# A two-layer decoder trunk: gating-unit projections moved ahead of the queries, four statistics moved in TensorE's queue, layer norm of the convolution one attention step earlier

## The chip, the cores and the metric

The kernel runs on one core of one Trainium2 chip. The metric is device time in microseconds of one execution. Before the change it is 2908.12 us, the median of three runs that lie between 2907.37 and 2908.25 us.

## What is computed

Two layers, each on 512 positions of width 1024, in fp32. Cut to what matters here:

```python
h = h + 0.5 * swiglu(rms(h), ffn1)
z = rms(h) @ w_in                      # one projection: columns for all mixers and gates
A = silu(layer_norm(causal_conv31(a * sigmoid(g)))) @ conv_out        # 512 channels
B = (u * (tril(ws) @ rms(v) + b)) @ sgu_out,   u, v = split(gelu(z_sgu))   # "gating unit"
C = nsa(z_q, z_kv, z_ngate) @ nsa_out  # 8 heads of 64, queries and keys RMS-normed,
                                       # three branches weighted by sigmoid(z_ngate)
h = h + (sig(g_A)*A + sig(g_B)*B + sig(g_C)*C) @ w_out
h = h + cross_attention(rms(h), rms(mem))
h = h + 0.5 * swiglu(rms(h), ffn2)
```

Everything lies transposed on the chip (channels on partitions, the 512 positions along the free side), so a statistic over channels is a matmul with a matrix of ones (`ones`, or `bdon` for heads of 64).

## The kernel before

**Units.** Every projection is cut into "units", one per 128 output columns: SP loads 1024 x 128 weights into `raw` (2 buffers), ScalarE copies their high part (`wH`, line 1083), GpSimd subtracts to get the low part (`wL`, line 563), TensorE does 24 matmuls of 512 columns (high x high, high x low, low x high for 8 slices, lines 616, 619 and 622; 12 for units with 4 slices), and VectorE takes the result out of one of 4 PSUM banks (`scaled`, line 1422, times the inverse RMS). ScalarE's `ahead(l, u)` prepares unit u + 3 as soon as unit u - 1 is done. The order of units within a layer is a table of offsets: `U_KV` (6 units), `U_CONV` (6), `U_QP` (4, the queries in pairs of heads), `U_NG` (2 half units, the gates of the attention branches), `U_SGU` (8: v then u of the gating unit), `U_CONV2` (2), and then `U_G`: 24 branch units (12 matmuls each) alternating with 24 gate units (24 matmuls each).

**Queues.** Each engine has a program in order, written out by hand in one block per engine (TensorE line 603, ScalarE line 1079, VectorE line 1412, GpSimd line 519, SP line 355). They are tied by counting semaphores: `stat_in` says that the squares for a statistic lie in `sacc`, `stat_mm` that TensorE has summed them, `stat_rt` that ScalarE has taken the root, `st_mm`/`st_out` count transposes on TensorE and their copies on ScalarE, `s_mm`/`s_out` scores and their readers on VectorE, `q_ok` normed queries, `vn` the normed v.

**Chain of a norm.** VectorE squares a tile into `sacc` (`squares`, line 1555), TensorE sums it (`stat`, line 628), ScalarE takes the root (`root`, line 1122), VectorE takes the reciprocal (`root_of`, line 1428) and multiplies (`normed`, line 1560). `sacc` and `rv` exist once, so these chains go one behind another. For v of the gating unit ScalarE makes the squares, TensorE sums the four of them (`v_squares`, line 759), and VectorE norms four tiles of 128 x 512 (line 1680).

**Pieces between matmuls.** From `U_CONV2` on, TensorE puts small work between the matmuls of the units. In the first four of these units `opening(p)` (line 890) is called after every 4 matmuls: transposes of v (`v_turned`), the mixing matmuls of the gating unit (`mixed`), the first scores. After that `attention(i, p)` (line 902) is called after every 2 matmuls, p = 0 to 17 within step i (branch unit i - 1 and gate unit i + 1): scores of step i, and transposes (`turned`) and value products (`values`) of step i - 1. There are 16 steps. Step i - 1 has 5, 2, 4 or 3 groups of transposes in turn.

**The order around the change.** ScalarE in step i: prepare a unit, copy out transposes 0 of step i - 1, the exponentials of half 0 of step i, copy out transposes 1, prepare a unit, and so on. VectorE in step i: row maxima of half 0 (`maxes`), the gate unit, convolution taps, maxima of half 1, the branch unit, weights (`weigh`), more taps. The convolution has 4 tiles of 31 taps: one is done by GpSimd (lines 577 to 594), the other three by VectorE (`conv(count)`, line 1593), where two of them accumulate in PSUM until their last taps. In steps 6 to 8 VectorE and ScalarE do the layer norm of the convolution: sum at step 6, mean taken off, squares and sum at step 7, root, reciprocal and product at step 8, then Silu and the high copies on ScalarE at the end of step 8, and `low("A", 4)` on VectorE; branch unit 8, which opens step 9, needs them.

Of the kernel before, what the change touches and what calls it, by code (L numbers as in the profile page):

```python
# [12 lines left out]
P = 128  # L13
# [4 lines left out]
def trunk(nc, x, mem, norm_ffn1, ffn1_wi, ffn1_wo, norm_mix, w_in, conv_w, conv_b, conv_ln_g,  # L18
# [38 lines left out]
    U_QP = U_CONV + 6  # L57
    U_NG = U_QP + 4
    U_SGU = U_NG + 2
    U_CONV2 = U_SGU + 8  # L60
# [10 lines left out]
    with ctx:  # L71
# [160 lines left out]
        def rows_of(u):  # L232
            if U_NG <= u < U_SGU or U_XO <= u < U_F2:
# [100 lines left out]
        q_ok = sig("q_ok", 1)  # L334
# [20 lines left out]
        def _(sp):  # L355
# [80 lines left out]
            with sp.Fori(0, L) as l:  # L436
# [13 lines left out]

                def pair_cols(j):
# [21 lines left out]
                for j in range(4):  # L473
                    unit(l, U_SGU + j, 0, cols_of(win, C_SGU + DS + j * P))
                for j in range(4):
                    unit(l, U_SGU + 4 + j, 0, cols_of(win, C_SGU + j * P))
# [42 lines left out]
        def _(pool):  # L519
# [52 lines left out]
            with pool.Fori(0, L) as l:  # L572
                lows(l, 0, U_QP)
# [3 lines left out]
                for u in range(U_QP, U_WO):  # L577
# [25 lines left out]
        def _(pe):  # L603
# [24 lines left out]
            def stat(l, s, weights, n=T):  # L628

                pe.wait_ge(stat_in, risen(stat_in, l, s + 1 if s < 9 else s))  # L630
# [56 lines left out]
            with pe.Fori(0, L) as l:  # L687
# [55 lines left out]
                unit(l, U_QP, 0, KD, gH, gL)  # L743
                for j in range(1, PAIRS):
                    unit(l, U_QP + j, 0, KD, gH, gL)
                    if j >= 2:
                        stat(l, 3 + j, bdon)
                for i in range(2):
                    unit(l, U_NG + i, 0, 4, lambda k: gxH[:, 4 * i + k, :],
                         lambda k: gxL[:, 4 * i + k, :])  # L750
                stat(l, 7, bdon)
                unit(l, U_SGU, 0, KD, gH, gL)

                pe.wait_ge(t_free, risen(t_free, l, 3))
                pe.wait_ge(ng_sig, risen(ng_sig, l, 1))
                for a in range(TT):
                    last = turn(pT[:, a * P:(a + 1) * P], hb[:, a * P:(a + 1) * P])
                last.then_inc(ng_tr, 1)
                def v_squares(k):
                    if k == 0:  # L760
                        pe.wait_ge(stat_rt, risen(stat_rt, l, 9))
# [4 lines left out]
                for j in range(1, 8):  # L766
                    unit(l, U_SGU + j, 0, KD, gH, gL)
                    if j == 1:
                        stat(l, 8, bdon)
                    if 2 <= j < 6:  # L770
                        v_squares(j - 2)


                def v_turned(c):
                    if c == 0:
                        pe.wait_ge(vn, risen(vn, l, 1))
                        pe.wait_ge(t_free, risen(t_free, l, 4))
# [6 lines left out]
                def mixed(c):  # L784

                    pe.wait_ge(sg_cp, risen(sg_cp, l, c + 1))
                    if c:
                        pe.wait_ge(sg_out, risen(sg_out, l, c))
# [6 lines left out]
                def scores(key):  # L795
# [3 lines left out]
                    else:  # L799
                        pe.wait_ge(q_ok, risen(q_ok, l, 1))  # L800
                    if isinstance(key, str):
                        j = int(key[1:])
                        for c in range(TT):
# [98 lines left out]
                def attention(i, p):  # L902
                    a, n = p // 3, len(groups(i - 1))
                    if p % 3 == 0:
                        if a < n:
                            turned(i - 1, a)
                        elif a == 5 and i == 6:
                            middle("mean", 10)
                        elif a == 5 and i == 7:
                            middle("var", 11)  # L910
# [5 lines left out]
                    elif 1 <= a <= n:  # L916
                        values(i - 1, a - 1)
# [161 lines left out]
        def _(act):  # L1079
# [72 lines left out]
            with act.Fori(0, L) as l:  # L1152
# [38 lines left out]
                ahead(l, U_QP)  # L1191
                for j in range(1, PAIRS):
                    ahead(l, U_QP + j)
                    if j >= 2:
                        root(l, 3 + j, rv, 1.0 / DH)
                ahead(l, U_NG)
                ahead(l, U_NG + 1)
                act.wait_ge(ng_in, risen(ng_in, l, 1))
                act.activation(hb, sr, ACT.Sigmoid).then_inc(ng_sig, 1)
                root(l, 7, rv, 1.0 / DH)  # L1200
                for j in range(8):
# [4 lines left out]
                    if j == 1:  # L1206
                        root(l, 8, rv, 1.0 / DH)
# [6 lines left out]
                    if j == 5:  # L1214
                        root(l, 9, rv, 1.0 / DS)
# [61 lines left out]
                exps_c(0)  # L1277
                v_out(3)
                exps(0, 0)
                ahead(l, gate_unit(0))  # L1280
# [9 lines left out]
                for i in range(1, NS + 1):  # L1290
# [13 lines left out]
                    ahead(l, branch_unit_of(i - 1))  # L1304
                    turned_out(i - 1, 0)
# [4 lines left out]
                    turned_out(i - 1, 1)  # L1310
                    ahead(l, gate_unit(i + 1))
# [9 lines left out]
                    if i == 6:  # L1321
                        act.wait_ge(st_mm, risen(st_mm, l, STEP["mean"] + 1))
                        copy(sil, pT, scale=-1.0 / DC).then_inc(st_out, 1)
                    if i == 7:
                        act.wait_ge(st_mm, risen(st_mm, l, STEP["var"] + 1))
                        act.activation(rv[:, :], pT, ACT.Sqrt, bias=eps[:, 0:1],
                                       scale=1.0 / DC).then_inc(st_out, 1)
                    if i == 8:
# [83 lines left out]
        def _(dve):  # L1412
# [116 lines left out]
            with dve.Fori(0, L) as l:  # L1529
# [109 lines left out]

                scaled(qT[:, 0, :], l, U_QP)  # L1640
                squares(qT[:, 0, :])
                conv(4)
                for j in range(1, PAIRS):
                    scaled(qT[:, j, :], l, U_QP + j)
                    if j >= 2:
                        normed(l, 3 + j, qT[:, j - 2, :], g8[:, j - 2:j - 1])
                        squares(qT[:, j - 1, :])
                    conv(3 if j == 1 else 1)
# [5 lines left out]
                normed(l, 7, qT[:, 2, :], g8[:, 2:3])  # L1654
                squares(qT[:, 3, :])
                conv(3)


                for j in range(8):
                    if j >= 2:  # L1660
                        dve.wait_ge(gelu, risen(gelu, l, j - 1))
                    scaled(tb[:, j % 2, :], l, U_SGU + j)
                    if j == 0:
                        dve.wait_ge(ng_tr, risen(ng_tr, l, 1))
                        dve.tensor_copy(gates[:, :, :], pT[:, :].rearrange("p (a c) -> p a c", a=4)
# [331 lines left out]
```

## Time and profile before

| what | value |
|---|---|
| median of the runs | 2908.12 us |
| the profiled execution | 2897.9 us, its span 2896.2 us |
| TensorE matmul busy | 2737.8 us (95%) |
| VectorE busy | 1213.8 us (42%) |
| ScalarE busy | 1159.7 us (40%) |
| GpSimd busy | 1223.7 us (42%) |

The profiled execution is 10.2 us below the median of the others. Times in rows are microseconds from the start of its span; in lines of the timeline the first number is the start, the second the duration, then engine, line, operation, the tiles written and read, and the count; in brackets how long the engine sat idle before it and what released it. PE is TensorE, DVE VectorE, ACT ScalarE, POOL GpSimd. The stretch in question lies at 476 to 800 us in the first layer and, 1430 us later, again in the second.

### The profile page before, as it was taken

The page shows a single profiled execution, that of the slowest core. Times are in us where ns is not written, and L with a number is a line of the kernel's source. Part 1 is how long each engine was busy: PE and PEld are TensorE (multiplying, and loading weights), DVE is VectorE, ACT ScalarE, POOL GpSimd, SP SyncE. Part 2 cuts the span into 40 slices and gives each one's busy share as a digit, 9 for nine tenths or more (in the row PEclk, how much of TensorE's full clock was granted, in tenths as well). Part 3 has the DMA queues.
Part 4 walks back from the last instruction along what each step waited for, and adds up shares of the span by engine and source line. Part 5 has one row for each costly group of instructions (what it writes and reads, how often), then busy time and mean ns, then how long its engine had stood idle before and what let it go on. Part 6 is the DMA issues. An engine that isn't in the chain of part 4 may idle for free.

```text
span 2896.2 us, 39971 instructions
## 1 busy us (share of the span) xinstructions
PE 2737.8 (95%) x13192; PEld 2153.7 (74%) x13192; DVE 1213.8 (42%) x1781; ACT 1159.7 (40%) x1682; POOL 1223.7 (42%) x624
## 2 busy tenths in 40 slices
PE   6999999899899989999999999998998999899999
PEld 5888877665567777888878888776555677688887
DVE  5222265776334554121242212667863346531212
ACT  4322332366764334222352223324667543342221
POOL 3443445752224424444444444467422344244443
PEclk8999999999999999999999999999999999999999
DMA  3335333221124313333333353332111332133332
GB/s 105 102 95 127 98 88 80 70 56 44 44 56 113 95 37 103 101 94 95 95 88 102 94 131 88 88 80 59 55 45 44 80 99 84 55 102 95 95 101 80
DMA packets 493189, 243.69 MB, mean 84 GB/s; under 512 B 49528, under 2 KB 491234, under 8 KB 493026
## 3 DMA queue, kind: packets, MB, share of 16 engines
q1 hardware_dynamic: 493026, 241.62, 30.0%
q8 instruction: 89, 1.46, 0.2%
q14 instruction: 74, 0.61, 0.1%
HBM read 239.46 MB, written 2.10 MB: 83 GB/s over the span
## 4 chain that ended last, share of the span: by engine, by line
issue 56%; POOL 25%; PE 12%; POOLq 7%; DVE 0%; DVEq 0%
POOL wL L563 24%; PE pg L616 4%; PE pg L619 4%; PE pg L622 4%; POOLq L589 3%; POOLq L591 3%; POOL wsn L587 1%; POOLq L562 1%; POOLq L568 0%; DVE big L1968 0%; POOL convb L584 0%; DVE xT L1475 0%; PE pg L667 0%; DVEq L71 0%; POOL tab L547 0%
## 5 line engine op out<-in xcount | busy, mean ns | idle before, releaser
L563 POOL TENSOR_TENSOR wL<-raw,wH 128x1024 fp32r<-128x1024 f32 (+1 forms) x480 | 1085.1, 2262 | 1637.2 <-ACT wH L1083 1634.2
L616 PE MATMUL pg<-gxH,wH 128*128 128x512 f32 x2320 | 938.0, 404 | 29.5 <-DVE gxL L1438 25.3
L622 PE MATMUL pg<-gxH,wL 128*128 128x512 f32 x2320 | 917.9, 396 | 0.0
L619 PE MATMUL pg<-gxL,wH 128*128 128x512 f32 x2320 | 916.1, 395 | 0.0
L1083 ACT ACTIVATE wH<-raw 128x1024 fp32r<-128x1024 f32 (+1 forms) x480 | 475.7, 991 | 487.7 <-PE pg L622 352.5
L616 PEld LDWEIGHTS pg<-gxH,wH 128*128 128x128 f32 x2320 | 440.0, 190 | 146.3 <-DVE gxL L1438 28.7
L619 PEld LDWEIGHTS pg<-gxL,wH 128*128 128x128 f32 x2320 | 440.5, 190 | 104.8 <-issue 18.8
L622 PEld LDWEIGHTS pg<-gxH,wL 128*128 128x128 f32 x2320 | 439.8, 190 | 94.6 <-issue 4.5
L616 PE MATMUL pg<-hH,wH 128*128 128x512 f32 (+1 forms) x1184 | 456.7, 386 | 20.7 <-DVE hL L1778 20.7
L622 PE MATMUL pg<-hH,wL 128*128 128x512 f32 (+1 forms) x1184 | 455.9, 385 | 0.0
L619 PE MATMUL pg<-hL,wH 128*128 128x512 f32 (+1 forms) x1184 | 454.0, 383 | 0.0
L616 PEld LDWEIGHTS pg<-hH,wH 128*128 128x128 f32 x1184 | 225.9, 191 | 64.9 <-DVE hL L1778 22.4
L1475 DVE SCALAR_TENSOR_TENSOR xT<-pg,xT 128x512 f32<-128x512 f32 x128 | 88.4, 691 | 432.3 <-PE pg L622 432.3
L619 PEld LDWEIGHTS pg<-hL,wH 128*128 128x128 f32 x1184 | 225.4, 190 | 55.2 <-issue 14.4
L622 PEld LDWEIGHTS pg<-hH,wL 128*128 128x128 f32 x1184 | 225.7, 191 | 37.8
L1083 ACT ACTIVATE hH<-tmp 128x512 f32 x88 | 55.6, 632 | 305.1 <-DVE tmp L1490 305.1
L1490 DVE TENSOR_TENSOR tmp<-pg,tmp 128x512 f32<-128x512 f32 x88 | 60.9, 692 | 255.1 <-PE pg L622 252.7
L1485 DVE TENSOR_TENSOR tb<-pg,rstd 128x512 f32<-128x512 f32 x88 | 60.8, 690 | 247.3 <-PE pg L622 245.9
L1136 ACT ACTIVATE tmp<-tb 128x512 f32<-128x512 f32 x88 | 55.5, 631 | 259.9 <-DVE tb L1485 259.9
L1241 ACT ACTIVATE prob<-prob,nb 128x512 f32<-128x512 f32 (+3 forms) x128 | 70.9, 555 | 91.6 <-DVE nb L1740 91.4
L1494 DVE TENSOR_TENSOR hL<-tmp,hH 128x512 f32 x88 | 70.0, 796 | 82.5 <-ACT hH L1083 82.5
L1487 DVE TENSOR_TENSOR tmp<-tmp,rstd 128x512 f32<-128x512 f32 x88 | 72.0, 818 | 74.1 <-ACT tmp L1136 74.1
(214 smaller groups left out, 2180.0 us busy)
## 6 DMA issues: line engine op xcount, KB each, us to landing
raw<-in_ffn_wi SPq DMA_DIRECT2D x352, 256.0 KB, 3.1
raw<-in_w_in SPq DMA_DIRECT2D x200, 256.0 KB, 3.2
raw<-in_ffn_wo SPq DMA_DIRECT2D x128, 256.0 KB, 3.0
raw<-in_ffn_wo SPq DMA_DIRECT2D x64, 192.0 KB, 2.6
raw<-in_w_out SPq DMA_DIRECT2D x32, 256.0 KB, 3.1
raw<-in_xkv SPq DMA_DIRECT2D x32, 256.0 KB, 3.1
raw<-in_sgu_out SPq DMA_DIRECT2D x32, 128.0 KB, 2.2
raw<-in_conv_out SPq DMA_DIRECT2D x32, 128.0 KB, 2.2
```

What stands on the lines that cost most here:

```text
L563: pool.tensor_tensor(wL[:, s % 4, 0:n, :], raw[:, s % 2, 0:n, :], wH[:, s % 4, 0:n, :].bitcast(F32), ALU.subtract)\
L589: pool.drain()
L591: pool.drain()
L616: mm(o, wH[:, s, k, :], rh(k), start=(k == 0), stop=False)
L619: mm(o, wH[:, s, k, :], rl(k), start=False, stop=False)
L622: last = mm(o, wL[:, s, k, :], rh(k), start=False, stop=(k == kt - 1))
L1083: return act.activation(o, i, ACT.Copy, **kw)
L1241: act.activation(t, t, ACT.Exp, bias=nb[:, s % 2, b, e:e + 1], scale=-1.0, accum_out=dn[:, s % 2, b, e:e + 1])
L1475: STT(xT[:, k, :], bank, by, xT[:, k, :], ALU.mult, ALU.add).then_inc(evac, 1)
L1487: TTt(sr, sil, rstd[:, :], ALU.mult)
L1490: TTt(hb, bank, sr, ALU.mult).then_inc(evac, 1)
L1494: TTt(hL[:, slot, :].rearrange(flat), hb, hH[:, slot, :].rearrange(flat).bitcast(F32), ALU.subtract).then_inc(hid_l, 1)
```

## The change

Nothing is computed differently. The eight units of the gating unit now stand ahead of the four query units. The v statistic becomes the first of this stretch; the statistics of the query pairs follow their projections one pair later, the last one as a piece of `opening`. The transposed branch gates also become a piece of `opening`. VectorE's queue follows: the norm of v comes right behind query unit 0, the norm of query pair 2 opens the stretch behind the gates, and that of pair 3 stands behind `weigh_c(0)`, with four taps, ahead of step 1. The taps are 5 instead of 4 at a time in steps 1 to 4. In the layer norm the sum moves to the end of step 5, the mean and squares to the end of step 6, reciprocal and product to step 7, Silu and the high copies to the end of ScalarE's step 7, `low("A", 4)` to the middle of VectorE's step 8. On TensorE the matmul of the mean stands at p = 6 of step 6, that of the variance at p = 0 of step 7, ahead of that step's transposes, which all move up by three pieces.

```diff
-    U_QP = U_CONV + 6
+    U_SGU = U_CONV + 6
+    U_QP = U_SGU + 8
     U_NG = U_QP + 4
-    U_SGU = U_NG + 2
-    U_CONV2 = U_SGU + 8
+    U_CONV2 = U_NG + 2
...
         for i in range(1, NS + 1):
+            if i == 7:
+                order.append("var")
             for g in range(len(groups(i - 1))):
...
-            if i == 7:
-                order.append("var")
...
-        q_ok = sig("q_ok", 1)
+        q_ok = sig("q_ok", PAIRS)
...
# TensorE
+                unit(l, U_SGU, 0, KD, gH, gL)
...
+                for j in range(1, 8):
+                    unit(l, U_SGU + j, 0, KD, gH, gL)
+                    if 3 <= j < 7:
+                        v_squares(j - 3)
                 unit(l, U_QP, 0, KD, gH, gL)
                 for j in range(1, PAIRS):
                     unit(l, U_QP + j, 0, KD, gH, gL)
                     if j >= 2:
-                        stat(l, 3 + j, bdon)
+                        stat(l, 4 + j, bdon)
...
-                stat(l, 7, bdon)
+                stat(l, 8, bdon)
...
                 def opening(p):
-                    if p in (0, 3, 6, 9):
-                        v_turned(p // 3)
-                    if p in (5, 8, 11, 14):
-                        mixed(p // 3 - 1)
+                    if p in (0, 3, 6, 10):
+                        v_turned((0, 3, 6, 10).index(p))
+                    if p in (5, 9, 12, 15):
+                        mixed((5, 9, 12, 15).index(p))
                     if p == 1:
                         scores("c0")
+                    if p == 4:
+                        gates_turned()
                     if p == 7:
+                        pe.wait_ge(sg_out, risen(sg_out, l, 1))
+                        stat(l, 9, bdon)
+                    if p == 8:
                         scores((0, 0))
...
                 def attention(i, p):
                     a, n = p // 3, len(groups(i - 1))
+                    g = a - 1 if i == 7 else a
                     if p % 3 == 0:
-                        if a < n:
-                            turned(i - 1, a)
-                        elif a == 5 and i == 6:
+                        if i == 7 and a == 0:
+                            middle("var", 11)
+                        elif g < n:
+                            turned(i - 1, g)
+                        elif i == 6 and a == n:
                             middle("mean", 10)
-                        elif a == 5 and i == 7:
-                            middle("var", 11)
...
# ScalarE, in step i
                     ahead(l, branch_unit_of(i - 1))
+                    if i == 7:
+                        act.wait_ge(st_mm, risen(st_mm, l, STEP["var"] + 1))
+                        act.activation(rv[:, :], pT, ACT.Sqrt, bias=eps[:, 0:1],
+                                       scale=1.0 / DC).then_inc(st_out, 1)
                     turned_out(i - 1, 0)
...
                     turned_out(i - 1, 1)
+                    if i == 6:
+                        act.wait_ge(st_mm, risen(st_mm, l, STEP["mean"] + 1))
+                        copy(sil, pT, scale=-1.0 / DC).then_inc(st_out, 1)
...
                     merge_gate(i)
-                    if i == 6:
...
-                    if i == 8:
+                    if i == 7:
                         for k in range(KB):
                             act.wait_ge(ln_sc, risen(ln_sc, l, k + 1))
                             act.activation(cacc[:, k, :], cacc[:, k, :], ACT.Silu,
...
# VectorE
+                for j in range(8):
+                    if j >= 2:
+                        dve.wait_ge(gelu, risen(gelu, l, j - 1))
+                    scaled(tb[:, j % 2, :], l, U_SGU + j)
+                    conv(5)
                 scaled(qT[:, 0, :], l, U_QP)
+                root_of(l, 5, rv)
+                for k in range(4):
+                    STT(vG[:, k, :], vG[:, k, :], col(P_SG + k), rv[:, :], ALU.mult, ALU.mult)
+                dve.drain().then_inc(vn, 1)
                 squares(qT[:, 0, :])
+                scaled(qT[:, 1, :], l, U_QP + 1)
                 conv(4)
+                scaled(qT[:, 2, :], l, U_QP + 2)
+                normed(l, 6, qT[:, 0, :], g8[:, 0:1])
+                squares(qT[:, 1, :])
+                scaled(qT[:, 3, :], l, U_QP + 3)
+                conv(2 * CONV_W if not held else len(held), True)
+                dve.drain().then_inc(q_ok, 1)
+                normed(l, 7, qT[:, 1, :], g8[:, 1:2])
+                dve.drain().then_inc(q_ok, 1)
+                squares(qT[:, 2, :])
...
                 low("B", 0)
                 gate(0)
                 weigh_c(0)
+                normed(l, 9, qT[:, 3, :], g8[:, 3:4])
+                dve.drain().then_inc(q_ok, 1)
+                conv(4)
 
                 for i in range(1, NS + 1):
...
                     gate(i)
                     if i < 6:
-                        conv(4)
+                        conv(5)
+                    if i == 7:
+                        dve.wait_ge(st_out, risen(st_out, l, STEP["var"] + 1))
+                        dve.reciprocal(rv[:, :], rv[:, :])
...
+                    if i == 8:
+                        low("A", 4)
+                    if i < NS:
+                        maxes(i, 1)
+                    branch(i - 1)
...
+                    if i < 5:
+                        conv(5)
+                    if i == 5:
                         conv(KB * CONV_W)
...
-                    if i == 7:
+                    if i == 6:
                         dve.wait_ge(st_out, risen(st_out, l, STEP["mean"] + 1))
```

## Rows read from the trace of the kernel before

**Rows 1.** Waits of TensorE from 476 to 800 us: in total, times, longest (us).
```profile
PE pg L616 <- DVE hL L1778: 10.3, 2, 10.0
...
PE pA L763 <- ACT sq L1213: 5.0, 1, 5.0
```

**Rows 2.** Busy time by stretch, first layer; behind POOL's stands the granted clock.
```profile
533.00:542.00 9.00, 9.00 (x26) 6.53 (x27) 8.53 (x10) 4.20 (x5) 5.38 (x4) 0.68 0.22 58
...
573.20:582.00 8.80, 8.74 (x50) 7.10 (x51) 2.79 (x6) 3.06 (x5) 6.81 (x6) 0.82 0.24 62
...
749.00:755.00 6.00, 5.96 (x22) 4.42 (x23) 4.17 (x11) 5.60 (x12) 2.37 (x1) 0.60 0.01 1
```

**Rows 3.** Timeline of TensorE: query statistics, v statistics, first transpose of v.
```profile
500.61 1.13 PE L631 MATMUL pA<-sacc,bdon 128*128 128x512 f32 x2 [1.62 <-DVEq L1426]
508.86 1.12 PE L631 MATMUL pA<-sacc,bdon 128*128 128x512 f32 x2 [1.64 <-DVEq L1426]
...
548.46 1.02 PE L763 MATMUL pA<-sq,ones 128*128 128x512 f32 x2
554.81 1.02 PE L763 MATMUL pA<-sq,ones 128*128 128x512 f32 x2
573.26 1.12 PE L667 MATMUL pA<-ident,big 128*128 128x128 f32 x4 [5.60 <-DVEq L1682]
```

**Rows 4.** Timeline of VectorE: units `U_CONV` + 2 and + 3, a query norm, taps, v's norm.
```profile
460.03 0.69 DVE L1422 TENSOR_TENSOR tb<-pg,rstd 128x512 f32<-128x512 f32 x1 [3.36 <-PE pg L622]
465.47 0.69 DVE L1422 TENSOR_TENSOR tb<-pg,rstd 128x512 f32<-128x512 f32 x1 [4.75 <-PE pg L622]
...
494.26 3.35 DVE L1431 RECIPROCAL rv<-rv 128x512 f32<-128x512 f32 x1 [0.89 <-ACT rv L1125]
...
498.93 1.60 DVE L1557 TENSOR_TENSOR sacc<-qT 128x512 f32<-128x512 f32 x1
...
555.62 4.06 DVE L1608 SCALAR_TENSOR_TENSOR pA<-convb,par,pA 128x512 f32<-128x512 f32 x5
...
566.38 6.80 DVE L1680 SCALAR_TENSOR_TENSOR big<-big,par,rv 128x512 f32<-128x512 f32 x4
```

**Rows 5.** VectorE: last row of `weigh_c(0)`, and taps in steps 2 and 3.
```profile
610.15 0.42 DVE L1728 TENSOR_TENSOR pc<-pc,wc 128x248 f32<-128x248 f32 x1
...
635.73 2.90 DVE L1608 SCALAR_TENSOR_TENSOR convb<-convb,par 128x512 f32<-128x512 f32 x4
...
641.34 5.87 DVE L1608 SCALAR_TENSOR_TENSOR convb<-convb,par 128x512 f32<-128x512 f32 x4
```

**Rows 6.** ScalarE in step 1: transposes 1, copied behind the exponentials.
```profile
613.68 0.60 ACT L1083 ACTIVATE sq<-pA 128x512 f32<-128x512 f32 x1 [0.16 <-issue]
```

**Rows 7.** TensorE: transposes 2 of step 1, 0 of step 7, 1 of step 8, branch unit 8.
```profile
614.34 0.66 PE L667 MATMUL pA<-ident,prob 128*128 128x128 f32 x4
...
704.01 0.65 PE L667 MATMUL pA<-ident,prob 128*128 128x128 f32 x4 [1.16 <-ACT tmp L1083]
...
727.87 0.60 PE L667 MATMUL pA<-ident,prob 128*128 128x128 f32 x4
...
749.04 0.80 PE L616 MATMUL pg<-hH,wH 128*128 128x512 f32 x1 [10.01 <-DVE hL L1778]
```

**Rows 8.** VectorE: end of `weigh(6)`; layer norm from mean to squares; the products.
```profile
699.13 0.16 DVE L1755 TENSOR_TENSOR wv<-wv,gates 128x4 f32<-128x4 f32 x1
...
707.32 2.49 DVE L1828 TENSOR_TENSOR convb<-convb,tmp 128x512 f32<-128x512 f32 x4
...
715.40 0.69 DVE L1835 TENSOR_TENSOR sacc<-sacc,tmp 128x512 f32<-128x512 f32 x1
...
732.41 2.67 DVE L1843 TENSOR_TENSOR convb<-convb,rv 128x512 f32<-128x512 f32 x4
```

**Rows 9.** ScalarE: the Silu of the layer norm, and the high copies behind it.
```profile
744.64 2.92 ACT L1332 ACTIVATE convb<-convb,par 128x512 f32<-128x512 f32 x4
747.63 2.19 ACT L1083 ACTIVATE hH<-convb 128x512 fp32r<-128x512 f32 x4
```

More of the change, by code:

```diff
@@ L449, in _ @@
                     conv_cols(U_CONV + 2 * j, j)
+                for j in range(4):
+                    unit(l, U_SGU + j, 0, cols_of(win, C_SGU + DS + j * P))
+                for j in range(4):
+                    unit(l, U_SGU + 4 + j, 0, cols_of(win, C_SGU + j * P))
                 def pair_cols(j):
@@ L572, in _ @@
             with pool.Fori(0, L) as l:
-                lows(l, 0, U_QP)
+                lows(l, 0, U_SGU)
                 pool.wait_ge(cin_in, risen(cin_in, l, 1))
                 k, o, term = 0, cacc[:, CT, :], wsn[:, :, :].rearrange("p g t -> p (g t)")
-                for u in range(U_QP, U_WO):
+                for u in range(U_SGU, U_WO):
                     low(l, u)
@@ L767, in _, with gates_turned @@
                     unit(l, U_SGU + j, 0, KD, gH, gL)
[L768 to L771, printed above, removed]
+                    if 3 <= j < 7:
+                        v_squares(j - 3)
+                unit(l, U_QP, 0, KD, gH, gL)
+                for j in range(1, PAIRS):
+                    unit(l, U_QP + j, 0, KD, gH, gL)
+                    if j >= 2:
+                        stat(l, 4 + j, bdon)
+                for i in range(2):
+                    unit(l, U_NG + i, 0, 4, lambda k: gxH[:, 4 * i + k, :],
+                         lambda k: gxL[:, 4 * i + k, :])
+                stat(l, 8, bdon)
+                def gates_turned():
+                    pe.wait_ge(sg_cp, risen(sg_cp, l, 2))
+                    pe.wait_ge(ng_sig, risen(ng_sig, l, 1))
+                    for a in range(TT):
+                        last = turn(pT[:, a * P:(a + 1) * P], hb[:, a * P:(a + 1) * P])
+                    last.then_inc(ng_tr, 1)
                 def v_turned(c):
@@ L1190, in _ @@
                     conv_gate(U_CONV + 2 * j, j)
[L1191 to L1200, printed above, removed]
                 for j in range(8):
@@ L1213, in _ @@
                         act.activation(sq[:, k % 2, :], vG[:, k, :], ACT.Square).then_inc(vsq, 1)
-                    if j == 5:
-                        root(l, 9, rv, 1.0 / DS)
+                ahead(l, U_QP)
+                root(l, 5, rv, 1.0 / DS)
+                for j in range(1, PAIRS):
+                    ahead(l, U_QP + j)
+                    if j >= 2:
+                        root(l, 4 + j, rv, 1.0 / DH)
+                ahead(l, U_NG)
+                ahead(l, U_NG + 1)
+                root(l, 8, rv, 1.0 / DH)
+                act.wait_ge(ng_in, risen(ng_in, l, 1))
+                act.activation(hb, sr, ACT.Sigmoid).then_inc(ng_sig, 1)
                 def v_out(c):
@@ L1277, in _ @@
                 exps_c(0)
+                root(l, 9, rv, 1.0 / DH)
                 v_out(3)
+                ahead(l, gate_unit(0))
                 exps(0, 0)
-                ahead(l, gate_unit(0))
                 conv_gate(U_CONV2, 3)
@@ L1784, in pair_low @@
                         hH[:, BR["C"] + j, :].bitcast(F32), ALU.subtract).then_inc(c_l, 1)
+                normed(l, 8, qT[:, 2, :], g8[:, 2:3])
+                dve.drain().then_inc(q_ok, 1)
+                squares(qT[:, 3, :])
                 maxes_c(0)
@@ L1788, in _ @@
                 scaled(tb[:, 0, :], l, U_CONV2)
+                dve.wait_ge(ng_tr, risen(ng_tr, l, 1))
+                dve.tensor_copy(gates[:, :, :], pT[:, :].rearrange("p (a c) -> p a c", a=4)
+                                [:, :, 0:NG])
+                dve.drain()
+                cmp0 = gates[:, 0, 0:NG:3]
+                TS(cmp0, cmp0, valid[:, 0:1], None, ALU.mult).then_inc(t_free, 1)
                 mixed(0)
@@ L1837, in _ @@
                         stat_given(None)
-                    if i == 8:
-                        dve.wait_ge(st_out, risen(st_out, l, STEP["var"] + 1))
-                        dve.reciprocal(rv[:, :], rv[:, :])
-                        dve.drain()
-                        for k in range(KB):
-                            TTt(cacc[:, k, :], cacc[:, k, :], rv[:, :], ALU.mult)\
-                                .then_inc(ln_sc, 1)
-                    if i < NS:
-                        maxes(i, 1)
-                    branch(i - 1)
-                    if i < NS:
-                        if i % TT == 0:
-                            weigh_c(i // TT)
-                        weigh(i)
-                        if i % TT == TT - 1 and i // TT + 1 < PAIRS:
-                            maxes_c(i // TT + 1)
-                    if i < 6:
-                        conv(4)
-                    if i == 8:
-                        low("A", 4)
                 def merged_low(m):
```

87 lines of the change are left out of this document (21 added, 66 removed).

## The prediction

> **What bounds the kernel.** The page comes first: TensorE is busy 95% of the span, so an edit that leaves its matmuls alone can only take away waits, add waits, or change the clock. The view of TensorE's waits over the stretch comes next: the longest are branch unit 8 waiting for the layer norm, and the v statistic waiting for ScalarE's squares [rows 1]. TensorE's timeline has the others ahead of step 1: two query statistics and the first transpose of v, which waits 5.60 us for VectorE's norm [rows 3]. Windows show what a long wait costs besides: 0.68 of the full clock over the 9 us behind the v statistic, 0.82 over 8.8 us behind the transpose, 0.60 over 6 us behind branch unit 8, part of each at 1.2 GHz, so 2.9, 1.6 and 2.4 us more [rows 2]. Long waits and their clock thus cost some 27 us per layer (5.0 + 5.6 + 10.0 + 6.9), the rest of the stretch's waits less. The change goes for all three. The question is what is late in their place, and that is read from VectorE's and ScalarE's queues [rows 4 to 9].
>
> **Part 1, up to the first transpose of v.** A unit takes 5.44 us (465.47 - 460.03) [rows 4], one with a statistic 6.35 (554.81 - 548.46) [rows 3], so a statistic costs 0.9. Unit U_CONV + 3 is taken at 465.5, so the first gating unit at 481.8, and query unit 0, eight units and four statistics on, at 529.0. The v statistics now come two units behind their tile, so their 5.0 us wait goes. The norm of v then falls where the queries' chain was. VectorE: reciprocal 3.4, four products 6.8, squares 1.7 up to TensorE's statistic (500.61 - 498.93) [rows 3, 4]: 541.9. TensorE is there after two more units, at 539.7: **wait 2.2**. Next: query copy 0.8, four taps 3.2 (4.06 / 5 each) [rows 4], copy 0.7, reciprocal and product 4.7 (498.93 - 494.26) [rows 4], squares 1.7: 553.0, against TensorE at 548.4: **wait 4.6**. From one query statistic to the next VectorE and ScalarE need 8.25 us [rows 3]; TensorE has 6.6 us of work there (8.25 - 1.64), so **wait 1.8** including the one tap: 561.4. The first transpose of v stands a statistic and 4 matmuls behind: 563.4 instead of 573.3, 9.9 us earlier. It no longer waits, since v has been ready since 540.
>
> In the opening pieces the gates' transpose (0.5) and the last statistic (1.0) are new. VectorE frees the transposes' bank only behind squares, c scores and the copy of CONV2: I estimate 1.2 us of wait at p = 6 and 0.6 at p = 7. Against that the old clock loss of 1.6 goes [rows 2]. At step 1 the kernel is 9.9 + 1.6 - 1.5 - 1.8 = **8 us** ahead. The DMAs, ScalarE's copies and GpSimd's low parts of the moved units cost nothing: a unit is prepared three units, 16 us, ahead, and every wait above lengthens that.
>
> **Part 2, steps 1 to 4.** Behind `weigh_c(0)` VectorE now norms query pair 3 (3.4 + 1.2) and does four taps before the maxima of step 1. Nobody needs pair 3 until step 12, but ScalarE copies out transposes 1 only behind the exponentials that need these maxima [rows 6], and transposes 2 need that copy. Taps with both tensors in SBUF took 0.73 us each at one place and 1.47 at another [rows 5]; I take 1.0. The block is 8.7 us. On the old clock VectorE comes out of `weigh_c(0)` at 610.6 [rows 5], so maxima end at 620.0, exponentials 1.1 and copy 0.7 and their hand-overs later 622.9 against TensorE at 614.3 [rows 7]: **wait 8.6**, and 2.4 us of clock behind it, as behind branch unit 8 [rows 2]. A fifth tap per call costs 1 us at the end of step 2 and 1 us at the start of step 4, where VectorE was last already. Together +13 us.
>
> **Part 3, layer norm.** At step 6 VectorE is free at 699.3, 1.1 later with the mean's matmul ahead of the scores: 700.4. From mean to squares it takes 8.8 us (707.32 to 716.1) [rows 8]: 709.2. The variance matmul stands at p = 0 of step 7, where TensorE is at 704.01 - 1.16 = 702.9 [rows 7]: **wait 6.3**, with the whole of TensorE's queue behind it. Then ScalarE's queue sets the pace. From the variance: root, gate copy, reciprocal, products 2.7 [rows 8] and maxima, 11.2 us; last exponentials and copy 1.6; weights 2.0; sigmoid 1.9; the Silu block 2.9 + 2.2 [rows 9] + 1.3 for its table; unit 1.1; copy 0.6: 24.8, so 734.0. Transposes 1 of step 8 wait for that copy; they stood at 727.9 [rows 7]. TensorE alone would take 20 us for this stretch (23.9 less 3.8 of waits and clock), so it waits **4.8**, less if the clock has fallen. From there to branch unit 8 it had 11.2 us of work (749.04 - 10.01 - 727.87), and 1.1 more for late exponentials: 746.3 without a wait, against 749.0 and 2.4 of clock: **5.1 us gained**.
>
> **Sum.** -8 + 13 - 5.1 = -0.1 us per layer, -0.2 for two, against the profiled execution 2897.9 us: 2897.7. The median of runs is 10.2 us above that execution; moved by as much, the forecast is 2908, and I put it at 2907, since each clock loss I charged is at the upper end of what one wait cost.
>
> **Rule against row.** The four products of v took 1.70 us each, with GpSimd busy in that window [rows 4], and taps on SBUF tensors 0.73 or 1.47 [rows 5]. The sum above takes the dear value for v and squares, 1.0 for taps. The Trainium skill, SBUF — State Buffer, "Who interferes with whom", says that a VectorE instruction with two SBUF inputs contends with a GpSimd instruction that reads SBUF. By that rule ScalarE's roots, late behind TensorE's waits, also leave GpSimd idle and v's norm cheaper than its old row, which is the first rival.
>
> **Rivals.** (1) *VectorE's chains run at their cheap price.* Products of v at half of 6.8 (-3), three squares at 0.8 instead of 1.6 (-2.4), the block's taps at 0.73 (-1.2), one square in the layer norm (-0.8): 7.4 us per layer, 2893. For it: GpSimd has less to do per unit beside the half units. Against: it still takes taps between units. (2) *The promised gain holds*, nothing takes the waits' place: 27 us less 1.5 of new pieces per layer, 2857; half of it 2882. Against it stand rows 6 and 8: two queues in order with long work ahead of what TensorE wants. (3) *Slower: taps become the pace of steps 1 to 4.* Ten taps at 1.47 [rows 5] and 4.6 us of other VectorE work make 19.3 us in a step that lasts 13.4; it decides above 0.9 us per tap. Price: 1.9 in the block, some 4 in step 2, 1 in step 3: 7 us per layer, 2921. The clock after the 4.6 us wait would add up to 2.9, of which the next wait hides 1.8. (4) *The change only moves waits that were hidden anyway*: it can't be, since the 10.01 us stand on TensorE itself.
>
> **Numbers.** Forecast as summed: 0.36, 2902 to 2913. Rival 1: 0.27. Rival 2, whole or half: 0.08. Rival 3: 0.29. What a measurement here can tell from no change is 0.2%, 5.8 us. So faster 0.35, same 0.36, slower 0.29. From 2885 to 2925 leaves out rival 2's whole and the far ends of the others.
>
> **What would show it.** In the trace after: no wait at v's statistic and first transpose; waits of 2, 5 and 2 us at the query statistics; some 9 us at transposes 2 of step 1, released by ScalarE's copy; 6 us at the variance; 2 to 5 at transposes 1 of step 8; none at branch unit 8. If step 1 shows no such wait, part 2 is wrong and the kernel is faster by 20 us or more. If steps 2 to 4 last over 18 us each, rival 3 is right.

## The result, and the profile after

The kernel after takes 2910.8 us (median of 20 runs, 2898.1 to 2917.0), the kernel before beside it 2903.8 us (20 runs, 2894.7 to 2914.7): ratio 1.0027, 95% interval [1.0018, 1.0037]. It is slower by some 7 us. That lies inside the range, but on the other side of the 0.2% line than the likeliest case. That 2910.8 is so near the predicted 2907 is luck: the forecast was reckoned from 2908.1 for the kernel before, which over 20 runs takes 2903.8.

The profiled execution took 2917.0 us, its span 2915.3 us. First, TensorE's waits over the whole kernel (in total, times, longest, us):

```profile
PE pA L668 <- ACT sq L1092: 42.8, 30, 7.8
...
PE pA L876 <- DVEq L1433: 14.5, 2, 7.2
```

The waits of [rows 1] are gone: 10.0 us at branch unit 8 and 5.0 us at the v statistic. In their place stand ScalarE's copy of turned probabilities, 7.8 us at worst, and the variance matmul of the layer norm (L876), 7.2 us in each layer. TensorE's timeline in the first layer says where:

```profile
548.92 1.13 PE L632 MATMUL pA<-sacc,bdon 128*128 128x512 f32 x2
559.55 2.08 PE L632 MATMUL pA<-sacc,bdon 128*128 128x512 f32 x2 [4.02 <-DVEq L1433]
568.74 1.12 PE L632 MATMUL pA<-sacc,bdon 128*128 128x512 f32 x2
570.63 0.60 PE L668 MATMUL pA<-ident,big 128*128 128x128 f32 x4
...
581.17 0.66 PE L668 MATMUL pA<-ident,big 128*128 128x128 f32 x4 [1.38 <-DVE gates L1789]
...
606.91 0.66 PE L668 MATMUL pA<-ident,prob 128*128 128x128 f32 x4 [1.98 <-ACT prob L1092]
...
620.90 1.11 PE L668 MATMUL pA<-ident,prob 128*128 128x128 f32 x4 [7.78 <-ACT sq L1092]
...
722.19 2.07 PE L876 MATMUL pA<-sacc,ones 128*128 128x512 f32 x2 [7.24 <-DVEq L1433]
...
748.72 1.11 PE L668 MATMUL pA<-ident,prob 128*128 128x128 f32 x4 [5.04 <-ACT sq L1092]
...
766.29 0.94 PE L668 MATMUL pA<-ident,prob 128*128 128x128 f32 x4 [1.71 <-ACT sq L1092]
...
805.87 1.08 PE L809 MATMUL pA<-kcn,qT 64*128 64x31 f32 x16
```

These are the statistics of query pairs 0, 1 and 2, the first and third transposes of v, transposes 0 and 2 of step 1 (each step counts its groups of transposes from 0), the variance, transposes 1 of step 8, transposes 1 of step 9, and the scores of the last compressed pair in step 11. The clock behind each wait stands ahead of the last two columns (granted clock, DMA share, GB/s):

```profile
559.50:570.00 10.50, 10.45 (x30) 0.73 0.20 52
...
604.00:621.00 17.00, 6.39 (x36) 0.86 0.13 32
621.00:634.00 13.00, 13.00 (x71) 0.79 0.07 20
...
741.00:749.00 8.00, 2.96 (x13) 0.81 0.00 0
749.00:762.00 13.00, 12.83 (x61) 0.85 0.23 62
```

**How to compare.** The two traces can't be laid over each other: at unit `U_CONV` + 3, still ahead of the changed part, the kernel after is already 9.1 us late (474.56 against 465.47 [rows 4]). That has nothing to do with the change (last section). So the first layer is cut at three places that every kernel has: VectorE's taking of unit `U_CONV` + 3, transposes 0 of step 1, and the scores of the last compressed pair. From the first to the second is the **head**, on to the third is the **tail**. The start of the head in after, then the ends of head and tail in before (those of after stand above):

```profile
474.56 0.69 DVE L1429 TENSOR_TENSOR tb<-pg,rstd 128x512 f32<-128x512 f32 x1 [4.75 <-PE pg L623]
```

```profile
607.93 0.66 PE L667 MATMUL pA<-ident,prob 128*128 128x128 f32 x4 [1.80 <-ACT prob L1083]
...
792.18 1.08 PE L806 MATMUL pA<-kcn,qT 64*128 64x31 f32 x16
```

Head of before 607.93 - 465.47 = 142.5 us, of after 606.91 - 474.56 = 132.4 us: **10.1 us won**. Tail of before 792.18 - 607.93 = 184.3 us, of after 805.87 - 606.91 = 199.0 us: **14.7 us lost**. Net 4.6 us in the first layer. The second layer, cut at the same places, has 1895.22, 2038.68 and 2222.70 in before, 1913.38, 2045.45 and 2242.18 in after: 11.4 us won in the head, 12.7 us lost in the tail, net 1.3. Both layers make 5.9 us, about what the medians say.

All kernels, e1 to e9 timed in 5 rounds beside the kernel before (e1, e2, e5 and e6 ran 12 times, e4 8 times, the others 6), with head and tail of the profiled execution, first layer / second layer:

| kernel | median us | ratio to before, 95% interval | head | tail |
|---|---|---|---|---|
| before | 2903.8, 2899.9, 2899.9, 2899.6 in four batches | | 142.5 / 143.5 | 184.3 / 184.0 |
| after | 2910.8 | 1.0027 [1.0018, 1.0037] | 132.4 / 132.1 | 199.0 / 196.7 |
| e1_ln_alone | 2901.5 | 0.9997 [0.9985, 1.0009] | 144.8 / 143.3 | 185.2 / 185.2 |
| e2_ln_back | 2909.4 | 1.0021 [1.0008, 1.0035] | 132.4 / 132.3 | 197.9 / 197.7 |
| e3_pair3_late | 2890.1 | 0.9946 [0.9927, 0.9964] | 131.9 / 132.4 | 189.3 / 189.4 |
| e4_both | 2891.1 | 0.9950 [0.9932, 0.9969] | 131.7 / 132.3 | 187.6 / 188.1 |
| e5_norm_late | 2899.6 | 0.9991 [0.9977, 1.0005] | 132.4 / 132.3 | 194.5 / 194.8 |
| e6_taps_late | 2903.9 | 1.0006 [0.9988, 1.0024] | 132.4 / 132.4 | 193.8 / 193.7 |
| e7_copies_late | 2883.3 | 0.9941 [0.9920, 0.9962] | 132.4 / 131.4 | 187.3 / 186.7 |
| e8_var_later | 2883.0 | 0.9929 [0.9912, 0.9946] | 132.4 / 132.0 | 187.0 / 187.2 |
| e9_three | 2876.5 | 0.9912 [0.9894, 0.9931] | 132.4 / 132.4 | 184.7 / 185.8 |

The two layers of one kernel differ by up to 2.2 us. The head of e1, which its edit doesn't touch, is 2.3 us longer than that of before in layer 1 and 0.2 us shorter in layer 2. So a difference of 1 or 2 us counts only where both layers show it.

One of the 8 runs of e4_both took 6914 us; the ratio leaves it out, and nothing explains it.

### The profile page after: what moved, and what is told of

Read it like the earlier page. It is cut to its first block, busy times and chain, and to the rows that moved or that the text cites. A ratio compares the mean times of both kernels' runs of the same rounds, so it can differ in the third digit from the quotient of the medians.

```text
span 2915.3 us, 39977 instructions
## 1 busy us (share of the span) xinstructions
PE 2754.6 (94%) x13192; PEld 2167.7 (74%) x13192; DVE 1195.3 (41%) x1781; ACT 1152.5 (40%) x1676; POOL 1218.1 (42%) x624
## 4 chain that ended last, share of the span: by engine, by line
issue 56%; POOL 24%; PE 12%; POOLq 7%; DVE 0%; DVEq 0%
POOL wL L564 24%; PE pg L617 4%; PE pg L620 4%; PE pg L623 4%; POOLq L590 3%; POOLq L592 3%; POOL wsn L588 1%; POOLq L563 1%; POOLq L569 0%; DVE big L1970 0%; POOL convb L585 0%; DVE xT L1482 0%; PE pg L668 0%; DVEq L71 0%; POOL tab L548 0%
```

## The experiments

### e1_ln_alone and e2_ln_back: the layer norm by itself

The first is the kernel before with only the layer norm moved up; the second is the kernel after with only the layer norm put back.

```diff
 # TensorE, step 7: e1 as after, e2 as before
-                        elif a == 5 and i == 7:
-                            middle("var", 11)
+                        if i == 7 and a == 0:
+                            middle("var", 11)
 # and with it the mean in step 6, the sum, squares and products on
 # VectorE, root and Silus on ScalarE, each one step
```

> The kernel before with the layer norm alone moved one step up. Theory L (read from the trace after): the move gives nothing by itself, because the wait of 10.0 us at branch unit 8 comes back as 7 us at the variance in step 7, 4 to 5 us at transposes 1 of step 8 and 1.7 us in step 9; the time is 0 to +6 us against before, ratio 1.000 to 1.002. Rival P (the prediction's part 3): 5 us gained per layer, ratio 0.9965. If the stall only shows when steps 1 to 4 are crowded with taps, the waits here are under 3 us each and the ratio is below 0.995.

> The changed kernel with the layer norm put back where it was. Theory L: the layer norm's move cost 1 to 2 us per layer, so 2 to 4 us come off the changed kernel: ratio to before about 1.001 to 1.002, and branch unit 8 waits some 8 to 10 us again. Rival P: putting it back costs 5 us per layer, ratio 1.006.

In e1 TensorE waits at the variance, at transposes 1 of step 8 and at transposes 1 of step 9, and not at branch unit 8:

```profile
720.89 2.08 PE L873 MATMUL pA<-sacc,ones 128*128 128x512 f32 x2 [7.24 <-DVEq L1427]
...
747.13 0.92 PE L667 MATMUL pA<-ident,prob 128*128 128x128 f32 x4 [3.57 <-ACT sq L1084]
...
764.23 0.96 PE L667 MATMUL pA<-ident,prob 128*128 128x128 f32 x4 [1.71 <-ACT sq L1084]
```

In e2 the old wait is back, and that of step 1 is there without the moved layer norm (here 5.83 us, 7.79 in layer 2):

```profile
612.76 1.11 PE L668 MATMUL pA<-ident,prob 128*128 128x128 f32 x4 [5.83 <-ACT sq L1091]
...
753.06 0.80 PE L617 MATMUL pg<-hH,wH 128*128 128x512 f32 x1 [10.17 <-DVE hL L1768]
```

On top of before the move costs 1.0 us of tail in layer 1 and 1.2 in layer 2; on top of e2 it costs 1.1 in layer 1 and wins 0.9 in layer 2. That is no gain and hardly a loss, and Theory L holds. Timed, e1 can't be told from before, nor e2 from after, and both intervals leave out what rival P asked for (0.9965 and 1.006). 10 us of wait at branch unit 8 were traded for 12.5 us in three pieces (7.24 + 3.57 + 1.71), less the short waits of steps 7 and 8 that went. The loss of tail, 13.6 us in e2 (13.7 in layer 2), comes from ahead of the layer norm.

### e3_pair3_late and e4_both: the block ahead of step 1

```diff
                 weigh_c(0)
-                normed(l, 9, qT[:, 3, :], g8[:, 3:4])
-                dve.drain().then_inc(q_ok, 1)
-                conv(4)
...
+                    if i == 5:
+                        normed(l, 9, qT[:, 3, :], g8[:, 3:4])
+                        dve.drain().then_inc(q_ok, 1)
                     if i < 5:
                         conv(5)
                     if i == 5:
                         conv(KB * CONV_W)
```

e3 is this on the kernel after, e4 is this on e2.

> The changed kernel with the norm of query pair 3 moved from ahead of step 1 into step 5, and without the four taps ahead of step 1. Theory Q: the 7.8 us at transposes 2 of step 1 are VectorE's 9 us block and nothing else; they go, and with them some 2 us of clock: 8 to 10 us per layer less than the changed kernel, ratio to before 0.995 to 0.998. Rival: the taps set the pace of steps 1 to 4, the wait comes back in steps 2 to 4, and at most 5 us in all come off: ratio 1.001 or more.

> The changed kernel with both: the layer norm back in its old place and the norm of pair 3 in step 5. If both theories hold, the parts add up: 18 us from the late pair and 3 from the layer norm, less the deeper wait at branch unit 8 that an earlier arrival brings (up to 5 per layer): ratio to before 0.993 to 0.997. If the layer norm's move pays only once TensorE arrives early, this is slower than the kernel with the late pair alone.

In after, VectorE's block between `weigh_c(0)` and the maxima of step 1 reads:

```profile
609.29 3.35 DVE L1438 RECIPROCAL rv<-rv 128x512 f32<-128x512 f32 x1
612.71 0.75 DVE L1570 SCALAR_TENSOR_TENSOR qT<-qT,g,rv 128x512 f32<-128x512 f32 x1
613.58 1.55 DVE L1615 SCALAR_TENSOR_TENSOR convb<-convb,par 128x512 f32<-128x512 f32 x1
615.05 0.92 DVE L1613 TENSOR_SCALAR convb<-convb,par 128x512 f32<-128x512 f32 x1
616.04 2.26 DVE L1615 SCALAR_TENSOR_TENSOR convb<-convb,par 128x512 f32<-128x512 f32 x2
618.48 0.06 DVE L1728 MEMSET nb<- 128x2 f32 x1 [0.18 <-issue]
```

It lasts 9.2 us (618.48 - 609.29), and the maxima that ScalarE's exponentials need start behind it. With the block away, transposes 2 of step 1 wait for nothing, and in step 1 of e3 two waits are left:

```profile
604.69 0.66 PE L668 MATMUL pA<-ident,prob 128*128 128x128 f32 x4 [1.98 <-ACT prob L1092]
...
618.51 0.41 PE L668 MATMUL pA<-ident,pc 128*31 128x128 f32 x2 [1.12 <-ACT sq L1092]
```

The tail falls by 9.7 us (199.0 to 189.3), in layer 2 by 7.4, and the kernel to 2890, 0.54% under before, a little more than theory Q expected; the rival is out. e4 is the same within the interval (2891), though its old wait at branch unit 8 is there again (10.16 us). Its tail is 1.7 and 1.2 us shorter than that of e3: with the block away, too, moving the layer norm up wins nothing.

### e5_norm_late and e6_taps_late: the block in halves

e5 moves only the norm of pair 3 and keeps the 4 taps; e6 drops only the `conv(4)`, so that those taps fall to the call at the end of step 5.

```diff
 # e5
-                normed(l, 9, qT[:, 3, :], g8[:, 3:4])
-                dve.drain().then_inc(q_ok, 1)
                 conv(4)
 # e6
                 normed(l, 9, qT[:, 3, :], g8[:, 3:4])
                 dve.drain().then_inc(q_ok, 1)
-                conv(4)
```

> The kernel after, with only the norm of query pair 3 moved from ahead of step 1 to the end of step 5 on VectorE; the 4 taps beside it stay. Theory Q (VectorE runs the block ahead of step 1 one piece after another, and the wait of 7.8 us at transposes 2 of step 1 is its tail): the wait shrinks by the 4.1 us of reciprocal and product, to 3 to 4 us, and the time falls by 8 to 10 us in two layers against the kernel after (2899 to 2902 beside about 2909), half of what leaving both pieces out gave. Theory C (what costs is that the clock falls whenever there is any wait there): a wait of 3 to 4 us still brings the lower clock, and only the 4.1 us themselves come back. Theory N (the taps, which read the same memory, are what is dear): under 4 us gained.

> The kernel after, with the norm of pair 3 ahead of step 1 as it is and only the 4 taps there left to the end of step 5. Theory Q: the wait at transposes 2 of step 1 shrinks by the 4.7 us that those taps take in the kernel after, to about 3 us, and the time falls by 9 to 11 us in two layers (2898 to 2901 beside about 2909). If the reciprocal, not the taps, is what makes the maxima late: no change, 2907 to 2911.

Transposes 0 and 2 of step 1 in e5, then transposes 2 in its layer 2, and a window ahead of the first of these waits (granted clock third from the end):

```profile
599.46 0.90 PE L668 MATMUL pA<-ident,prob 128*128 128x128 f32 x3 [1.98 <-ACT prob L1092]
...
610.46 1.11 PE L668 MATMUL pA<-ident,prob 128*128 128x128 f32 x4 [2.71 <-ACT sq L1092]
...
2041.36 1.11 PE L668 MATMUL pA<-ident,prob 128*128 128x128 f32 x4 [4.78 <-ACT sq L1092]
```

```profile
600.00:602.00 2.00, 2.00 (x9) 1.21 (x7) 1.78 (x6) 1.99 (x3) 0.00 (x0) 0.50 0.00 0
```

The same two transposes in e6:

```profile
598.74 0.66 PE L668 MATMUL pA<-ident,prob 128*128 128x128 f32 x4 [1.99 <-ACT prob L1092]
...
607.91 0.72 PE L668 MATMUL pA<-ident,prob 128*128 128x128 f32 x4 [2.96 <-ACT sq L1092]
```

The waits by themselves mislead. In layer 1 of e5 the clock had already fallen ahead of the wait (0.50 from 600 to 602 us), so TensorE came late and waited only 2.71 us; in layer 2, on the full clock up to the wait, it waited 4.78. The distance from transposes 0 to transposes 2 says when ScalarE's copy came, as long as TensorE waits for it at all: 14.0 us in after, 11.0 in e5 and 9.2 in e6, each the same in both layers; with both parts away it is 6.7 us in e3 (8.0 in layer 2, on a lowered clock). So the late norm takes off 3.0 us and the late taps 4.8. The norm alone is 4.1 us long, but the four taps that stay took 6.0 us in e5, against 4.7 in after; why, no run shows.

Theory Q holds: each part of the block takes its share off. N falls, though the taps are the larger half. For theory C the picture is mixed: a lowered clock stands behind the wait in both (0.50 from 610 to 615 us in e5, 0.55 from 610 to 612 us in e6), but full again in e6 from 612 us on. The tail falls by 4.5 us in e5 and 5.2 in e6 in layer 1, by 1.9 and 3.1 in layer 2, against 9.7 and 7.4 with both parts away: in the first layer the halves add up, in the second they give less. Timed, e5 (2899.6) is clear of after, as expected; e6 (2903.9) gained less than the 9 to 11 us expected, and its interval overlaps that of after.

### e7_copies_late, e8_var_later, e9_three: the chain of the layer norm

All three build on e3. e7 moves the four high copies from behind the Silus at the end of step 7 into step 8, behind the second turned copy. e8 moves the variance matmul behind the first transposes of step 7. e9 does both.

```diff
 # e7, ScalarE
                     turned_out(i - 1, 1)
+                    if i == 8:
+                        for k in range(KB):
+                            copy(hH[:, BR["A"] + k, :], cacc[:, k, :]).then_inc(br_h, 1)
...
                         act.drain()
-                        for k in range(KB):
-                            copy(hH[:, BR["A"] + k, :], cacc[:, k, :]).then_inc(br_h, 1)
 # e8, TensorE in step 7; order and ScalarE's root follow
                         if i == 7 and a == 0:
+                            turned(6, 0)
+                        elif i == 7 and a == 1:
                             middle("var", 11)
```

> The kernel with pair 3 late, and on ScalarE the four copies of the normed convolution (2.7 us) moved from the end of step 7 to behind the second turned copy of step 8; the Silus stay. Theory S (the wait of 4.8 us at transposes 1 of step 8 is ScalarE's block of Silus and copies at the end of step 7): that wait falls to about 2.1 us, and the time by 5 us in two layers against 2890, to 2885. Theory V (VectorE's products, or the probabilities, are late anyway): the wait stays near 4.8 us with another releaser, time 2890.

> The kernel with pair 3 late, and the variance matmul of the layer norm behind the first transposes of step 7 instead of ahead of them, some 3.6 us of TensorE work later. Theory L (the move of the layer norm won nothing because the wait for the squares on VectorE took the place of the old wait): the variance wait falls from 7.2 to about 3.6 us and the time by 6 to 7 us in two layers, to 2884. Rival R (the end of the chain, from the variance over the Silus to transposes 1 of step 8, is fixed by VectorE and ScalarE, so that what is not waited for at the variance is waited for in step 8): the variance wait falls, the wait in step 8 grows by as much, time 2888 to 2891.

> Pair 3 late, the four copies of the normed convolution in step 8, and the variance matmul behind the first transposes of step 7, all three together. If the two moves in the layer norm act on different links of one chain that ends at transposes 1 of step 8, the sum of both gains holds only in part: the variance wait is 4.6 us as before, the wait at transposes 1 of step 8 falls from 4.0 to about 1.5 us, time 2877 to 2880. If they fully overlap, 2883 as either alone. If the copies, now beside the exponentials of step 8, make transposes 1 of step 9 late, above 2883.

Variance and transposes 1 of step 8 in e3, e7, e8 and e9, in this order, and for e9 transposes 0 and 1 of step 9 as well:

```profile
710.57 2.07 PE L876 MATMUL pA<-sacc,ones 128*128 128x512 f32 x2 [7.25 <-DVEq L1433]
...
737.41 1.12 PE L668 MATMUL pA<-ident,prob 128*128 128x128 f32 x4 [4.77 <-ACT sq L1092]
```

```profile
705.00 2.08 PE L876 MATMUL pA<-sacc,ones 128*128 128x512 f32 x2 [7.25 <-DVEq L1434]
...
729.32 1.12 PE L668 MATMUL pA<-ident,prob 128*128 128x128 f32 x4 [3.05 <-ACT sq L1092]
```

```profile
705.02 2.08 PE L876 MATMUL pA<-sacc,ones 128*128 128x512 f32 x2 [4.58 <-DVEq L1435]
...
729.05 1.12 PE L668 MATMUL pA<-ident,prob 128*128 128x128 f32 x4 [3.99 <-ACT sq L1094]
```

```profile
704.75 2.08 PE L876 MATMUL pA<-sacc,ones 128*128 128x512 f32 x2 [4.57 <-DVEq L1436]
...
726.77 0.66 PE L668 MATMUL pA<-ident,prob 128*128 128x128 f32 x4 [2.13 <-ACT sq L1094]
...
740.54 0.66 PE L668 MATMUL pA<-ident,prob 128*128 128x128 f32 x4 [1.04 <-ACT prob L1094]
...
744.92 0.66 PE L668 MATMUL pA<-ident,prob 128*128 128x128 f32 x4 [1.71 <-ACT sq L1094]
```

e7: the second wait falls by 1.7 us in layer 1 and by 3.5 in layer 2 (5.05 to 1.57), around the 2.7 us of the copies, and the tail by 1.9 and 2.6: theory S. e8: the first wait falls by 2.7 us in both layers (3.6 expected) and the second does not grow but falls by 0.8 and 0.4; the tail falls by 2.3 and 2.2. Rival R is out. e9: the tail falls by 4.5 and 3.6 us, against 4.2 and 4.8 for the two moves apart, so they act for the most part on links of their own. Transposes 1 of step 9, feared to come late, wait 1.71 us as in e3; new is 1.04 us at transposes 0 of that step.

These shares are read from one trace of each kernel. Timed over six runs each, e7 and e8 can't be told from e3, whose interval theirs overlap, and that of e9 only just touches it. At 2876.5 us and ratio 0.9912 e9 **beats both kernels**, and its wait at the variance is still 4.6 us.

## Why the prediction was right or wrong

**Part 1, forecast -8 us up to step 1; the head measured -10.1.** The waits at the v statistic and at the first transpose of v went as read from [rows 1, 3]: TensorE reaches that transpose at 570.63 - 9.1 = 561.5, forecast 563.4. In layer 2 the head measured -11.4. No run has the head's change alone, but the nine kernels that have it show the same head in both layers, 131.4 to 132.4 us, against 142.5 to 144.8 in before and e1. The three waits put at the query statistics (2.2, 4.6, 1.8) came as none, 4.02 and none. The term mis-sized is the four products of v: charged at 6.8 us [rows 4], they took 5.06. (The three terms that the prediction names for VectorE there end at 540.9 and not at 541.9; it doesn't name the copy of the query unit ahead of them.)

```profile
542.07 5.06 DVE L1655 SCALAR_TENSOR_TENSOR big<-big,par,rv 128x512 f32<-128x512 f32 x4
```

GpSimd, busy for 6.8 of 7.5 us around the old products, now stood idle for 1.1 us within them, since its half units are shorter than its whole ones. The Trainium skill, SBUF — State Buffer, "Who interferes with whom", says that a VectorE instruction with two SBUF inputs contends with a GpSimd instruction that reads SBUF; the trace agrees in that the products are shorter where GpSimd does less, but no run changes that alone. A piece of rival 1 held, and only this one: squares took 1.54 us, not 0.8, and the block's taps 1.2, not 0.73.

**Part 2, forecast +13 us; measured +13.6 and +13.7** (tail of e2 less tail of before). Block forecast 8.7, measured 9.2 us; wait forecast 8.6, measured 7.78 (7.14 in layer 2); clock behind it 0.79. The split was less exact than the sum: wait and clock of the block were put at 11 us and came to 10.3 and 9.5 (e2 less e4), the groups of five taps at 2 us and what is left came to 3.3 and 4.1 (e4 less before). The mechanism, VectorE's block in front of the maxima and ScalarE's copy behind the exponentials, is shown by e3, e5 and e6, which take it away whole and in halves. Rival 3 is out: taps took 1.2 us each in the block and 0.74 to 1.31 in the groups of five behind it, not 1.47, and steps 2 to 4 lasted 14.7, 17.1 and 18.7 us, of which only the last is over the 18 us that it asked for. A small piece of it holds: the groups cost 1 to 2 us more than forecast. Pair 3 is first needed by the scores in step 11, not 12, which changes nothing in the sum.

**Part 3, forecast -5.1 us; measured +1.1 and -0.9 in the two layers (after less e2), +1.0 and +1.2 (e1 less before). This step failed.** Its places were right: variance 7.24 (forecast 6.3), transposes 1 of step 8 5.04, 3.57 in layer 2 (forecast 4.8), none at branch unit 8. Its size was not, for two terms of the sum. The first is the waits. They add up to 14.0 us (12.5 in layer 2) with 1.71 us in step 9 that the forecast lacked, against 11.1 forecast. The second is the clock, which was booked on one side only: 2.4 us were taken back for the old wait, and nothing was charged for the two new ones, although [rows 2] showed a lowered clock behind every long wait. The windows above have 0.81 and 0.85 from 741 to 762 us.

Before and e1, which differ in nothing else, give both terms a size. Cut the tail into windows of 1 us, and add up TensorE's idle time, and for the clock its busy time times the missing share of the granted clock. The idle time is 21.1 and 19.9 us in the two layers of before, 20.0 and 20.0 in e1: 0.5 us less on average, where the forecast had 2.7 less (749.0 - 746.3). The clock costs 4.1 and 5.5 us in before, 6.3 and 6.2 in e1: 1.5 us more, where it had 2.4 less. The two errors of 2.2 and 3.9 us are the 6.1 us between -5.1 and the +1.1 that e1 measured, with the clock as the larger.

**The sum.** Forecast -8 + 13 - 5.1 = -0.1 us per layer; measured -10.1 + 13.6 + 1.1 = +4.6 in the first layer and -11.4 + 13.7 - 0.9, which is +1.3 before rounding, in the second. So errors of 2 to 3 us on one side and 4 to 6 us on the other made "no change" the likeliest case where the kernel is slower by 0.27%. Rival 2 is out: the head's gain came, but the block took it back, and the promised gain of the layer norm was given back whole.

**The level.** The forecast added the 10.2 us between profiled execution and median as they stood. They are about as large as one loss of the last section.

## What to carry to other kernels

A step that takes away one long wait should be summed with the clock on both sides: what the old wait cost behind it comes back, and every new wait of some microseconds is charged the same. Before something is moved into a gap of an in-order queue, look at who waits for the very next instruction there: 9.2 us of work that nobody needed for five steps (the taps) or ten (the norm) stood in front of maxima that were needed at once, and putting them where the queue had slack turned a loss of 0.27% into a gain of 0.54%. A chain split over three engines gives its time back only link by link: moving the whole chain up won nothing, moving two of its links against the others took 4.5 and 3.6 us off the tails of the two layers and brought the median of six runs from 2890.1 to 2876.5 us.

## What was not expected of the hardware

A stretch that the change doesn't touch, 256 small matmuls of the compression, ran at either level of TensorE's clock. In before and after:

```profile
422.57 3.92 PE L715 MATMUL pA<-big 64*64 64x31 f32 x128
426.32 3.90 PE L715 MATMUL pA<-big,convb 64*64 64x31 f32 x128
```

```profile
422.80 7.04 PE L716 MATMUL pA<-big 64*64 64x31 f32 x128
429.64 7.02 PE L716 MATMUL pA<-big,convb 64*64 64x31 f32 x128
```

In them the window says for before, and ahead of them and in them for after (busy time of PE, PEld, DVE, ACT, POOL, then the granted clock):

```profile
425.00:435.00 10.00, 10.00 (x201) 9.15 (x198) 2.12 (x3) 1.49 (x3) 2.40 (x1) 1.00 0.02 3
```

```profile
418.00:425.00 7.00, 5.18 (x52) 3.56 (x52) 6.23 (x6) 1.97 (x2) 0.00 (x0) 0.77 0.27 75
...
422.00:423.00 1.00, 1.00 (x8) 0.67 (x9) 0.82 (x1) 0.98 (x2) 0.00 (x0) 0.50 0.00 0
...
425.00:435.00 10.00, 10.00 (x194) 10.00 (x191) 1.89 (x3) 0.00 (x0) 0.00 (x0) 0.50 0.01 2
```

TensorE is busy all of those 10 us and gets the full clock of 2.4 GHz in before and 1.2 GHz in after. Idle time ahead of them is the same in both (5.19 and 5.18 of 7 us busy), but in after the clock fell there, to 0.50 from 422 us on, ahead of the first of these matmuls at 422.80; in before it stood at 1.00 throughout. It came back behind them: 0.50 up to 441 us and 0.69 from 441 to 443, in matmuls of 512 columns. The Trainium skill, TensorE: Matmul & The Clock Gate, "Part 1: The HAM clock gate", has activity release the throttle; here the trace doesn't agree for these small matmuls, in which an engine that the profile calls busy stays at the low level to their end.

Over the 11 profiled kernels and their two layers it was 8 passes of 22: both in after, none in before, e5, e7 and e9, one in each other. The loss was 6.2 us in the matmuls (14.06 - 7.82), and from the first of them to unit `U_CONV` + 3 8.9 us in layer 1 of after (9.1 less the 0.2 by which it was late already) and 7.3 us in layer 2. The times of the runs fall in groups at that distance: of before's 20, ten between 2894.7 and 2900.5, nine between 2907.2 and 2908.6, one at 2914.7. That these groups are none, one and two such losses fits, and in the batch of e9 the three runs of before over 2907 us have a mean granted clock of 0.976 to 0.977, the other eight 0.978 to 0.981; but where the clock was low only profiled executions show. The two losses are 16.2 of the 19.1 us between the spans of before and after, and none of it is the change. Why the clock falls in one pass and not in another wasn't tried.
